# A hybrid diffusion layer on one core: transposes and half of the first projection chunk moved into the modulation, `w_out` loaded without waiting, the second half of the modulation spread out, the query projection led by token block 0, 36 expert rows ahead in place of 20

## The chip, the cores and the metric

The kernel runs on one core of one Trainium2 chip, in float32 throughout. The metric is the time of one execution on the device in microseconds (us), as the median of several runs. Addresses into this document: a name such as L720 is line 720 of the kernel before; the lines of the kernel after are named only where rows of its instruction order are shown.

## The reference, cut to what matters

One layer over 256 latent tokens (x) and 256 context tokens (ctx), width 2048. `silu` is applied to the two condition vectors, a product with `w_mod` (2048 x 12288) gives six modulation rows for each.

```python
mod = silu(c) @ w_mod + b_mod; mod_c = silu(c_ctx) @ w_mod + b_mod
sh1, sc1, ga1, sh2, sc2, ga2 = split(mod, 6)
pc = modulate(rmsnorm(ctx, g_norm_mix), csh1, csc1) @ w_in       # 2048 x 4128
p  = modulate(rmsnorm(x, g_norm_mix), sh1, sc1) @ w_in
four, qk, v, o, gates = split_proj(p, b_gate)
y_m, _ = mlstm_mix(silu(conv_latent(qk)), v, o, gates, g_mlstm, ctx_states)  # 8 heads
y = concatenate([fourier_mix(four, g_fourier), y_m]) @ w_out     # 2048 x 2048
x = x + ga1 * y
h2 = modulate(rmsnorm(x, g_norm_ffn), sh2, sc2)

def peer(xb):                                   # per block of 128 tokens
    q = (xb @ w_query).reshape(128, 8, 2, 128)  # 8 heads, 2048 x 2048
    s = einsum('thpd,hpnd->thpn', q, sub_keys)
    sv, si = top_k(s, 16)                       # then 16 x 16 candidates per head
    top_s, pos = top_k(cand, 16); idx = take_along_axis(cidx, pos)
    act = gelu(einsum('thkd,td->thk', expert_u[idx], xb))
    return einsum('thk,thkd->td', softmax(top_s) * act, expert_v[idx])
out = rmsnorm(x + ga2 * peer(h2), g_final)
```

The last part is the bulk of the traffic: each of 256 tokens picks 8 x 16 experts, and each pick is one row of 8 KB of `expert_u` and one of `expert_v`, 537 MB together.

## The kernel before, in words

Every engine has its own hand-written program (SyncE `sp`, GpSimd `pool`, ScalarE `act`, TensorE `pe`, VectorE `dve`), and semaphores tie them together: `wait_ge` blocks that engine's program in order, so what stands behind a wait waits too. Nothing reorders the work at run time.

1. **Modulation, first third.** `load_moda` (L263) brings the first 4096 columns of `w_mod` in 16 pieces of 2 MB into four buffers; a piece waits until the one four before it is used (`w_free`). `partial_mod` multiplies each piece on TensorE, with 32 output rows at a time in four column groups (L654); `columns_of_mod` (L662) turns the result into columns. ctx and x come between the pieces, ScalarE sums their squares, VectorE scales them (`norm_tokens`).
2. **Transposes and H.** After the last piece, 16 transposes of 512 tokens (L682) go through PSUM; ScalarE (L451) and VectorE (L982) modulate them into `H`, which holds all tokens with the channels on partitions.
3. **Projection.** `w_in` is used in 8 chunks of 512 columns, each as two halves of the contraction (`kh`), 2 MB each, on two buffers `W[0]`, `W[1]`. Ahead of it stand the gates, 16 matmuls of 104 rows (L690). Chunks 3, 2, 4, 5 (L714, L716, L720) run straight through; the other four are cut in halves and laid between the heads of the mLSTM. Meanwhile VectorE computes the other 16 chunks of the modulation for x alone: `modb(m)` is 16 multiply-adds over a 4 MB chunk of `w_mod` (L929), which GpSimd loads into `W[2]`, `W[3]`; TensorE sums its 128 rows (L699, `reduce_modb`), and `modb_out` adds the bias. 12 of the 16 are done before the scans (`MODB_LATE`), with the convolutions between them, 4 beside `w_out`.
4. **mLSTM.** For each head TensorE does half a chunk of projection, `values(h-1)` (L773), `scores(h)` (L755); VectorE `diagonals`, `weigh`, `divide` (L1122), ScalarE the exponentials. Then `positions` (L795) and `channels` (L807) do the Fourier group.
5. **w_out.** SyncE waits for `y_ready` (L284) before it loads the first piece of `w_out`. TensorE transposes y (L831), then four chunks of 64 matmuls for both token blocks (L846); VectorE adds to x. Then the keys are transposed (L860), `h2` of both blocks is normed (L1206, L1209) and transposed (L868).
6. **Query.** Four chunks n of `w_query`, 64 matmuls each for both blocks together (L883), then the scores of two heads (L893). `pick(g, n)` on VectorE finds the 16 experts of a head of a token block (g is 0 to 15; 0 to 7 are block 0). The `w_query` pieces are loaded by SyncE (L253), each into the half buffer that was just used.
7. **Experts.** One rank r (0 to 255) is 16 ranks per pick. `gather_u(r)` (L374, an indirect DMA from GpSimd, 1 MB) brings 128 rows of `expert_u`, `dot(r)` on VectorE (L1273) multiplies them with h2, `weight_of(r)` on ScalarE makes a diagonal of the weights, and TensorE adds 128 rows of `expert_v` under it (L905, 4 matmuls of 512 columns, 8 instructions). `LEAD` ranks of U are gathered, on `EARLY` = 5 buffers, before the first V; the first V waits for `w_free` 48 and `score_psum` 8, that is for the whole query stage, because V's buffers are those of `w_query` and its sums lie in the same PSUM banks. From there two V go with one U until U is `LAG` = 4 ahead, then one with one, on 6 U and 7 V buffers.

In TensorE's rows a float32 matmul stands as two instructions (16 matmuls are x32).

## Time and profile before

| | |
|---|---|
| median of 3 runs | 2081.48 us (2077.37 to 2081.89) |
| the profiled execution: its own time, its span | 2078.71 us, 2076.7 us |
| TensorE busy | 1669.7 us (80%) |
| VectorE busy | 1111.1 us (54%) |
| ScalarE, GpSimd busy | 389.0 us, 669.2 us |
| moved by DMA | 723.54 MB, mean 348 GB/s |
| TensorE clock, mean granted | 0.969 |

The span is what the trace covers, from the first to the last instruction; times in the trace are counted from its start. Busy shares are means over stages with different limits, so the stages have to be read one by one. A granted clock of 1.00 is 2.4 GHz. The rows that matter stand in a section of their own below.

### The profile page before, as it was taken

To read this page: it belongs to the slowest core of one execution; us is meant where nothing else is said; L and a number is where in the kernel's file an instruction comes from. 1 tells how busy PE (TensorE), PEld (TensorE's weight loads), DVE (VectorE), ACT (ScalarE), POOL (GpSimd) and SP (SyncE) were. 2 spreads that over 40 slices of the span, in tenths; PEclk is the share of its full clock that TensorE was granted. 3 is DMA by queue.
4 is the path that set the end of the run, shared out by engine and by line. 5 is a ranking of instruction groups with operands and counts; after the bars stand their busy time and mean duration, and the time that the engine had idled before them with its cause. 6 is when DMAs were issued, how large, how long until landed. Compare 5 with 4: busy or idle time off the path is not lost.

```text
span 2076.7 us, 13923 instructions
## 1 busy us (share of the span) xinstructions
PE 1669.7 (80%) x4609; PEld 782.8 (38%) x4609; DVE 1111.1 (54%) x1856; ACT 389.0 (19%) x1126; POOL 669.2 (32%) x577
## 2 busy tenths in 40 slices
PE   4599999999699978998777777777777777777776
PEld 1155544556444767333222223222232232222222
DVE  0177996234454284164646646646647556556443
ACT  1110002113200102122212122122123122122111
POOL 1011100000000052554445345355354464454430
PEclk8799999999899999999999999999999999999999
DMA  9978887231766395999999999999999999999996
GB/s 379 408 286 314 309 301 270 96 107 62 262 245 222 122 360 235 420 402 423 423 422 424 423 424 423 423 423 424 423 423 421 424 423 423 423 423 423 423 423 252
DMA packets 136759, 723.54 MB, mean 348 GB/s; under 512 B 10202, under 2 KB 10538, under 8 KB 69619
## 3 DMA queue, kind: packets, MB, share of 16 engines
q0 software_dynamic: 92784, 614.83, 72.0%
q1 hardware_dynamic: 43744, 107.78, 14.1%
q8 instruction: 36, 0.59, 0.1%
q14 instruction: 33, 0.26, 0.0%
q10 hardware_dynamic: 162, 0.08, 0.0%
HBM read 720.52 MB, written 2.13 MB: 348 GB/s over the span
## 4 chain that ended last, share of the span: by engine, by line
DMA 42%; PE 33%; DVE 12%; POOL 8%; issue 3%; ACT 1%; DVEq 0%; SPq 0%; POOLq 0%; ACTq 0%
DMA ring<-in_expert_u,acc 24%; PE ps L720 11%; DMA qh<-in_expert_u,acc 8%; PE ps L846 5%; POOL ring L374 5%; PE ps L883 5%; DMA ring<-in_w_mod 4%; DVE ring L1273 3%; PE ps L714 3%; PE ps L905 3%; DMA ring<-in_expert_v,acc 2%; DMA ring<-in_w_query 2%; DMA modrow<-in_expert_v,acc 1%; PE ps L716 1%; POOL VX L374 1%
## 5 line engine op out<-in xcount | busy, mean ns | idle before, releaser
L905 PE MATMUL ps<-ring,wg 128*128 128x512 f32 x1184 | 545.1, 605 | 178.1 <-DMA ring<-in_expert_v,acc 177.7
L1273 DVE SCALAR_TENSOR_TENSOR ring<-ring,A 128x2048 f32<-128x2048 f32 x174 | 397.0, 2292 | 334.3 <-DMA ring<-in_expert_u,acc 334.0
L905 PEld LDWEIGHTS ps<-ring,wg 128*128 128x128 f32 x1184 | 216.0, 191 | 506.0 <-issue 270.2
L374 POOL DMA_INDIRECT ring<-in_expert_u,acc x174 | 216.8, 1246 | 446.5 <-DVE ring L1273 337.3
L905 PE MATMUL ps<-H,wg 128*128 128x512 f32 x576 | 266.7, 607 | 81.7 <-DMA H<-in_expert_v,acc 81.7
L604 ACT ACTIVATE wg<-K,VX 128x128 f32<-128x128 f32 x256 | 102.8, 402 | 711.8 <-PE ps L905 707.4
L720 PE MATMUL ps<-ring,H 128*128 128x512 f32 x512 | 223.4, 595 | 1.2 <-ACT VX L473 1.2
L374 POOL DMA_INDIRECT ring<-in_expert_v,acc x148 | 177.1, 1196 | 69.2 <-issue 43.6
L905 PEld LDWEIGHTS ps<-H,wg 128*128 128x128 f32 x576 | 105.2, 191 | 242.5 <-issue 134.4
L929 DVE SCALAR_TENSOR_TENSOR acc<-ring,vec,acc 128x512 f32<-128x512 f32 x240 | 180.5, 752 | 21.6 <-DMA ring<-in_w_mod 13.3
L905 PE MATMUL ps<-modrow,wg 128*128 128x512 f32 x288 | 133.6, 607 | 39.4 <-DMA modrow<-in_expert_v,acc 39.4
L324 POOL DMA_DIRECT2D ring<-in_w_mod x32 | 28.8, 899 | 365.9 <-DVE acc L929 265.7
L720 PEld LDWEIGHTS ps<-ring,H 128*128 128x128 f32 x512 | 96.1, 190 | 125.2 <-issue 123.1
L1273 DVE SCALAR_TENSOR_TENSOR VX<-VX,A 128x2048 f32<-128x2048 f32 x43 | 98.5, 2291 | 80.9 <-DMA VX<-in_expert_u,acc 80.8
L1273 DVE SCALAR_TENSOR_TENSOR qh<-qh,A 128x2048 f32<-128x2048 f32 x39 | 89.4, 2291 | 79.6 <-DMA qh<-in_expert_u,acc 79.6
L883 PE MATMUL ps<-H,ring 128*128 128x256 f32 x512 | 113.3, 383 | 13.9 <-DMA ring<-in_w_query 13.4
L846 PE MATMUL ps<-ring,H 128*128 128x512 f32 x256 | 112.4, 600 | 12.9 <-DMA ring<-in_w_out 12.9
L883 PEld LDWEIGHTS ps<-H,ring 128*128 128x128 f32 x512 | 98.0, 192 | 28.2 <-issue 12.3
L374 POOL DMA_INDIRECT VX<-in_expert_u,acc x43 | 64.6, 1503 | 121.3 <-DVE VX L1273 115.8
L905 PEld LDWEIGHTS ps<-modrow,wg 128*128 128x128 f32 x288 | 52.6, 192 | 119.8 <-ACT wg L604 60.9
L599 ACT ACTIVATE VX<-VX 128x1 f32<-128x1 f32 x256 | 51.4, 201 | 224.3 <-DVE ring L1273 147.6
L374 POOL DMA_INDIRECT H<-in_expert_v,acc x72 | 78.0, 1084 | 28.1 <-issue 21.0
(216 smaller groups left out, 1251.0 us busy)
## 6 DMA issues: line engine op xcount, KB each, us to landing
ring<-in_w_mod POOLq DMA_DIRECT2D x32, 2048.0 KB, 8.7
ring<-in_w_mod SPq DMA_DIRECT2D x16, 2048.0 KB, 21.3
ring<-in_w_in SPq DMA_DIRECT2D x16, 2048.0 KB, 11.7
ring<-in_w_out SPq DMA_DIRECT2D x8, 2048.0 KB, 11.0
ring<-in_w_query SPq DMA_DIRECT2D x8, 2048.0 KB, 11.5
ring<-in_expert_u,acc POOLq DMA_INDIRECT x174, 26.2
ring<-in_expert_v,acc POOLq DMA_INDIRECT x148
B<-in_ctx SPq DMA_DIRECT2D x2, 1024.0 KB, 25.5
```

Of the source, the lines that this page charges most:

```text
L324: pool.dma_start(W[2 + kh], wm[kh * KH * P:(kh + 1) * KH * P, bass.ds(m * CH + 2 * D, CH)].rearrange("(k p) n -> p k n", p=P)).then_inc(m_ ...
L374: nc.gpsimd.indirect_dma_start(rows_, None, table, bass.IndirectOffsetOnAxis(ap=eidx[:, rank:rank + 1], axis=0)).then_inc(loaded, 16)
L599: link(nc_a.activation(act_t[:, r:r + 1], dots[:, r:r + 1], ACT.Gelu_apprx_tanh))
L604: nc_a.activation(diag[:, r % 4, :], ident, ACT.Copy, scale=wgt[:, r:r + 1]).then_inc(S["diag_ready"], 1)
L714: ins = mm(bank, W[kh][:, k, j * P:(j + 1) * P], H[:, kk, :], **flags)
L716: ins = mm(bank[:, 0:T], W[kh][:, k, j * P:(j + 1) * P], H[:, kk, T:2 * T], **flags)
L720: ins = mm(bank, H[:, kk, b * P:(b + 1) * P], W[kh][:, k, :], **flags)
L846: ins = mm(ps[:, 2 * par + b, :], yT[:, kk, b * P:(b + 1) * P], W[kh][:, k, :], start=kk == 0, stop=kk == KB - 1)
L883: ins = mm(ps[:, 2 * (n % 2) + j // 2, (j % 2) * T:(j % 2 + 1) * T], W[kh][:, k, j * P:(j + 1) * P], h2T[:, kk, :], start=kk == 0 and j % ...
L905: ins = mm(ps[:, 4 * b + n, :], diag[:, r % 4, :], v_rows[r % V_SLOTS][:, n * CH:(n + 1) * CH], start=k == 0, stop=k == BLOCK_RANKS - 1, s ...
L929: ins = v.scalar_tensor_tensor(out=a, in0=W[2 + kh][:, k, :], scalar=s, in1=a, op0=ALU.mult, op1=ALU.add)
L1273: v.scalar_tensor_tensor(out=rows_u, in0=rows_u, scalar=1.0, in1=A[:, r // BLOCK_RANKS, :], op0=ALU.mult, op1=ALU.mult, accum_out=dots[:, ...
```

## The change

All of it is in the order of work; what is computed is the same.

- **Front.** The first third of the modulation is computed in another column order (shift and scale of the first 1024 channels first), so that `H` of the first eight channel blocks can be made while the second half still loads. TensorE then has transposes and `project_early` between the pieces: the first half (`kh` 0) of chunk 3 of `w_in`, whose 2 MB are loaded into `KT` and `qh` between `w_mod` pieces 7 and 8. The gates are computed in four column groups of 32 rows and summed by one more matmul.
- **Modulation, rest.** 8 chunks of `modb` ahead of the scans in place of 12; 3.5 chunks go as halves between `weigh(h)` and `divide(h)` of heads 0 to 6, a half behind them, 4 beside `w_out` as before.
- **w_out.** Its first two pieces are loaded as soon as the projection is done (`w_free` 32). TensorE begins with the half of the contraction that the mLSTM fills, ahead of the wait for `y_ready`. The last chunk is done for token block 0 first, then the keys are transposed, then block 1.
- **Query.** Block 0 is normed and modulated by itself, its two first heads are projected one by one with the tokens on the output rows (then transposed), and scored and picked before block 1 is there. Chunks 1 to 3 are as before, with `kh` 1 first.
- **Experts.** `LEAD` is 36 in place of 20; near the end `lag_behind` lets V come from 4 to 1 behind U.

```diff
-REDUCE_BEHIND = [1, 4, 6, 10, 15, 19, 22, 24, 26, 28, 31]
...
+REDUCE_BEHIND = [7, 9, 13, 17, 20, 23, 26, 29]
...
-LEAD = 20
+LEAD = 36
...
+CLOSING = 24
...
-MODB_EARLY, MODB_LATE = 1, 12
+MODB_SCAN, MODB_LATE = 8, 12
...
+def lag_behind(u):
+    return LAG if u < RANKS - CLOSING else LAG - (u - (RANKS - CLOSING)) // (CLOSING // LAG)
...
+        WE = [KT[:], qh[:].rearrange("p a b t -> p (a b t)").rearrange("p (k n) -> p k n", k=4)]
...
+            c0 = W_IN_CHUNKS[0] * CH
+            for i in range(2):
+                sp.dma_start(WE[i], wi[4 * i * P:4 * (i + 1) * P, c0:c0 + CH].rearrange(
+                    "(k p) n -> p k n", p=P)).then_inc(S["ld_we"], 16)
+            for piece in range(8, 4 * MODA_N):
+                load_moda(piece)
+            sp.wait_ge(S["w_free"], 14)
+            load(1, wi, 1, bass.ds(W_IN_CHUNKS[0] * CH, CH))
...
-            sp.wait_ge(S["y_ready"], 1)
-            for base, src in ((32, w_out[0]), (40, w_query[0])):
-                with sp.Fori(0, 4) as n:
-                    for kh in range(2):
-                        sp.wait_ge(S["w_free"], n * 2 + (base + kh - 1))
-                        load(kh, src, kh, bass.ds(n * CH, CH))
+            sp.wait_ge(S["w_free"], 32)
+            for kh in HALVES:
+                load(kh, w_out[0], kh, slice(0, CH))
+            for n in range(1, 4):
+                for i, kh in enumerate(HALVES):
+                    sp.wait_ge(S["w_free"], 32 + 2 * n + i - 1)
+                    load(kh, w_out[0], kh, slice(n * CH, (n + 1) * CH))
...
-            load_from(1, MODB_LATE + 1)
+            load_from(1, MODB_SCAN + 1)
             pool.dma_start(gy[:, 0:FW], g_fourier.to_broadcast([P, FW])).then_inc(S["ld_gy"], 16)
             pool.dma_start(gy[:, FW:D], g_mlstm.to_broadcast([P, FW])).then_inc(S["ld_gy"], 16)
+            load_from(MODB_SCAN + 1, MODB_LATE)
...
+            pool.wait_ge(S["score_psum"], 10)
             for i in range(LEAD - LAG):
                 gather_u(LEAD + i)
                 gather_v(2 * i)
                 gather_v(2 * i + 1)
-            for r in range(2 * (LEAD - LAG), RANKS - LAG):
-                gather_u(r + LAG)
-                gather_v(r)
-            for r in range(RANKS - LAG, RANKS):
-                gather_v(r)
+            r = 2 * (LEAD - LAG)
+            for u in range(r + LAG, RANKS):
+                gather_u(u)
+                while r + lag_behind(u) <= u:
+                    gather_v(r)
+                    r += 1
+            gather_v(RANKS - 1)
...
+            def project_early(first, last):
+                for step in range(first, last):
+                    j, k = step // KH, step % KH
+                    if j == 0:
+                        wait_ht(k)
+                    if step == 0:
+                        pe.wait_ge(S["ld_we"], 32)
+                    ins = mm(ps[:, 1 + j, :], WE[k // 4][:, k % 4, j * P:(j + 1) * P], H[:, k, :],
+                             start=k == 0, stop=False)
+                    if step == 4 * KH - 1:
+                        ins.then_inc(S["w_free"], 1)
...
+            transpose_x(0)
+            transpose_x(1)
+            columns_of_mod(1).then_inc(S["modcol_psum"], 1)
+            transpose_x(2)
+            partial_mod(2, 0)
+            for k in range(3, 6):
+                transpose_x(k)
+            partial_mod(2, 1)
+            for k in range(6, 8):
+                transpose_x(k)
+            project_early(0, 4)
+            partial_mod(2, 2)
+            project_early(4, 8)
+            partial_mod(2, 3)
+            project_early(8, 12)
+            pe.wait_ge(S["mod_ready"], 1)
...
+            project_early(15, 18)
+            partial_mod(3, 2)
+            project_early(18, 21)
+            partial_mod(3, 3)
+            transpose_x(8)
+            project_early(21, 24)
+            columns_of_mod(3).then_inc(S["modcol_psum"], 1)
+            transpose_x(9)
+            transpose_x(10)
+            project_early(24, 26)
...
+                pe.wait_ge(S["ld_wg"], 16)
+                for k in range(KB):
+                    g = 32 * (k % 4)
+                    ins = mm(ps[g:g + 32, 0, :], wg[:, k, :], H[:, k, :], start=k < 4,
+                             stop=k >= KB - 4)
...
+                mm(ps[0:NG, 0, :], gate_sel, gate_parts, start=True, stop=True
...
+                    if (i, kh, j) == (0, 1, 0):
+                        gate_parts_of_projection()
+                    if (i, kh, j) == (0, 1, 1):
+                        sum_gates()
...
+                if h >= 2 and h % 2 == 0:
+                    reduce_modb(MODB_SCAN + h // 2 - 1)
...
+            for i in range(KB // 2):
+                transpose_y(i)
+            pe.wait_ge(S["yT_ready"], KB // 2)
+            project_out(0, 0)
+            reduce_modb(MODB_LATE - 1)
+            pe.wait_ge(S["y_ready"], 1)
+            for i in range(KB // 2, KB):
+                transpose_y(i)
             pe.wait_ge(S["yT_ready"], KB)
...
+            for n in range(3):
+                if n >= 1:
+                    project_out(n, 0)
+                project_out(n, 1)
+                reduce_modb(MODB_LATE + n)
+            project_out(3, 0, (0,))
+            project_out(3, 1, (0,)).then_inc(S["out_tb0"], 1)
+            reduce_modb(MODB_LATE + 3)
...
+            project_out(3, 0, (1,))
+            project_out(3, 1, (1,))
...
+            def query_head(b, h, first, last):
+                for step in range(first, last):
...
+                    ins = mm(ps[:, h, 0:T], h2T[:, kk, b * P:(b + 1) * P],
+                             W[kh][:, k, h * T:(h + 1) * T], start=step == 0, stop=step == KB - 1)
...
+            pe.wait_ge(S["out_free"], 6)
+            query_head(0, 0, 0, KB)
+            pe.wait_ge(S["out_free"], 8)
+            transpose_h2(1, 0)
+            transpose_h2(1, 1)
+            query_columns(0, 0)
+            query_head(0, 1, 0, 4)
+            head_scores(0, 0)
+            query_head(0, 1, 4, KB)
...
+            query_head(1, 0, 0, 4)
+            head_scores(0, 1)
+            query_head(1, 0, 4, KH)
+            query_head(1, 1, 0, KH).then_inc(S["w_free"], 1)
+            query_head(1, 0, KH, KB)
+            query_head(1, 1, KH, KB)
+            query_columns(1, 0).then_inc(S["w_free"], 1)
+            head_scores(1, 0)
+            query_columns(1, 1)
+            head_scores(1, 1)
...
+                if h >= 2 and h % 2 == 0:
+                    modb_out(MODB_SCAN + h // 2 - 1)
+                if h < MH - 1:
+                    modb_half(MODB_SCAN + h // 2, h % 2)
                 divide(h)
...
+            modb_half(MODB_LATE - 1, 1)
...
+            dve.wait_ge(S["out_tb0"], 1)
+            add_mixed(3, 0)
+            modb_out(MODB - 1)
+            dve.wait_ge(S["g2_ready"], 1)
+            dve.wait_ge(S["ld_sh2"], 16)
+            modulate(0)
+            dve.wait_ge(S["w_free"], 40)
+            add_mixed(3, 1)
+            modulate(1)
...
+                if g == 0:
+                    dve.wait_ge(S["score_ready"], 5)
+                if g == SOFT_FIRST - 2:
+                    dve.wait_ge(S["score_ready"], 10)
+                if g + 2 < TB * PH:
                     pick(g + 2, g + 2)
```

How TensorE's order changes at the front. Before, behind the last `w_mod` piece (L654, ring) the columns (L662), then the 16 transposes (L682, B is ctx, A is x), the gates (L690), the sum of a `modb` (L699), then chunk 3 (L714):

```order
L654 MATMUL ps<-ring,acc 32x512 x32
L662 MATMUL ps<-K,VX 128x2 x16
L682 MATMUL ps<-K,B 128x128 x2
L682 MATMUL ps<-K,A 128x128 x2
...
L690 MATMUL ps<-H,wg 104x512 x16
L699 MATMUL ps<-acc,K 32x512
L714 MATMUL ps<-H,ring 128x512 x16
```

After, from the first early projection on (L774, weights in KT and qh), with the `w_mod` pieces (L742) and a set of columns (L751) between; the lower rows are the end of the early work, the first piece of chunk 3's second half (L861) and the gates (L828):

```order
L774 MATMUL ps<-H,KT 128x512 x4
L742 MATMUL ps<-ring,acc 32x512 x8
L774 MATMUL ps<-H,qh 128x512 x4
L742 MATMUL ps<-ring,acc 32x512 x8
L774 MATMUL ps<-H,KT 128x512 x4
L751 MATMUL ps<-K,VX 128x2 x8
L742 MATMUL ps<-ring,acc 32x512 x8
L774 MATMUL ps<-H,qh 128x512 x3
...
L774 MATMUL ps<-H,qh 128x512
L861 MATMUL ps<-H,ring 128x512 x8
L828 MATMUL ps<-H,wg 32x512 x16
```

The 32 matmuls of the first half have moved from behind the transposes to between the pieces of `w_mod` 10 to 15, and 16 matmuls of 104 rows have become 16 of 32 rows.

From the transposes of y to the first query chunk, TensorE before: L831 transposes y, L846 is `w_out`, L852 sums a `modb`, L860 transposes the keys, L868 h2, L883 is the query projection, L893 scores:

```order
L831 MATMUL ps<-K,A 128x128 x32
...
L846 MATMUL ps<-ring,H 128x512 x32
...
L852 MATMUL ps<-acc,K 32x512
...
L860 MATMUL ps<-K,gy 128x128 x16
L868 MATMUL ps<-K,A 128x128 x32
L883 MATMUL ps<-H,ring 128x256 x64
L893 MATMUL ps<-modrow,qh 128x128 x8
```

After: L980 transposes y, L992 is `w_out`, L844 sums a `modb`, L1020 transposes the keys, L1031 h2, L1053 projects one head of one block:

```order
L980 MATMUL ps<-K,A 128x128 x16
L992 MATMUL ps<-ring,H 128x512 x16
L844 MATMUL ps<-acc,K 32x512
L980 MATMUL ps<-K,A 128x128 x16
L992 MATMUL ps<-ring,H 128x512 x16
...
L992 MATMUL ps<-ring,H 128x512 x16
L844 MATMUL ps<-acc,K 32x512
L1020 MATMUL ps<-K,gy 128x128 x16
L992 MATMUL ps<-ring,H 128x512 x16
L1031 MATMUL ps<-K,A 128x128 x16
L1053 MATMUL ps<-ring,H 128x256 x16
```

What follows on TensorE, block 1's h2 (L1031) and block 0's second head, with the query of head 0 turned (L1061) and scored (L1071):

```order
L1031 MATMUL ps<-K,A 128x128 x8
L1061 MATMUL ps<-K,qtok 128x128 x2
L1053 MATMUL ps<-ring,H 128x256 x4
L1071 MATMUL ps<-modrow,qh 128x128 x2
L1053 MATMUL ps<-ring,H 128x256 x12
L1031 MATMUL ps<-K,A 128x128 x8
```

Half a chunk of `w_out` now stands between the two halves of y's transposes, the keys' transposes and one block's h2 stand around the last half chunk, and the first scores come behind 20 query matmuls in place of 64.

## Rows read from the trace of the kernel before

**Rows 1.** The page, part 2: the span in 40 slices of 51.9 us.
```profile
GB/s 379 408 286 314 309 301 270 96 107 62 262 245 222 122 360 235 420 402 423 423 422 424 423 424 423 423 423 424 423 423 421 424 423 423 423 423 423 423 423 252
```

**Rows 2.** Windows: length, busy by engine (PE, PEld, DVE, ACT, POOL), clock, DMA share, GB/s.
```profile
90.00:104.00 14.00, 9.21 (x48) 1.81 (x48) 0.00 (x0) 0.00 (x0) 0.00 (x0) 0.64 1.03 401
...
1000.00:2000.00 1000.00, 741.74 (x1600) 290.85 (x1600) 585.51 (x919) 220.37 (x663) 480.53 (x400) 0.99 1.01 423
```

**Rows 3.** Timeline of TensorE at the front: start, busy us, operation [idle before].
```profile
54.79 1.95 PE L654 MATMUL ps<-ring,acc 128*32 128x512 f32 x16 [1.83 <-DMA ring<-in_w_mod]
...
100.88 3.27 PE L654 MATMUL ps<-ring,acc 128*32 128x512 f32 x16 [2.41 <-DMA ring<-in_w_mod]
...
119.42 13.95 PE L690 MATMUL ps<-H,wg 128*104 128x512 f32 x32 [1.26 <-ACT H L451]
...
134.28 14.00 PE L714 MATMUL ps<-H,ring 128*128 128x512 f32 x32
...
192.84 7.50 PE L716 MATMUL ps<-H,ring 128*128 128x256 f32 x34
```

**Rows 4.** Timeline of TensorE, the half chunk ahead of the heads.
```profile
340.90 13.97 PE L720 MATMUL ps<-ring,H 128*128 128x512 f32 x32 [1.21 <-ACT VX L473]
354.80 0.44 PE L738 MATMUL ps<-K,gsb 40*128 40x40 f32 x4
```

**Rows 5.** Timeline of VectorE in a head, after the heads, beside w_out.
```profile
393.40 0.16 DVE L1122 COPY small<-ps 128x2 f32<-128x2 f32 x1 [10.14 <-PE ps L773]
...
527.30 0.25 DVE L1156 RECIPROCAL st<-st 128x16 f32<-128x16 f32 x1 [15.13 <-ACT st L541]
...
640.85 11.78 DVE L929 SCALAR_TENSOR_TENSOR acc<-ring,vec,acc 128x512 f32<-128x512 f32 x15
```

**Rows 6.** Timeline of TensorE from the Fourier stage to the last scores.
```profile
494.58 3.70 PE L795 MATMUL ps<-K,A 128*128 128x512 f32 x8
...
531.93 6.24 PE L831 MATMUL ps<-K,A 128*128 128x128 f32 x32 [4.32 <-DVE A L1160]
...
551.12 29.23 PE L846 MATMUL ps<-ring,H 128*128 128x512 f32 x64 [12.94 <-DMA ring<-in_w_out]
...
684.84 27.89 PE L883 MATMUL ps<-H,ring 128*128 128x256 f32 x128 [0.52 <-ACT H L573]
...
758.92 15.76 PE L883 MATMUL ps<-H,ring 128*128 128x256 f32 x64 [12.13 <-DMA ring<-in_w_query]
...
822.00 2.05 PE L893 MATMUL ps<-modrow,qh 128*128 128x128 f32 x16 [1.16 <-ACT qh L583]
```

**Rows 7.** Timeline of VectorE and GpSimd in the query stage.
```profile
715.71 0.29 DVE L1234 COPY QT<-H 128x256 f32<-128x256 f32 x1 [34.82 <-ACT H L589]
...
727.07 0.29 DVE L1234 COPY QT<-H 128x256 f32<-128x256 f32 x1
...
751.54 2.29 DVE L1273 SCALAR_TENSOR_TENSOR ring<-ring,A 128x2048 f32<-128x2048 f32 x1 [0.96 <-DMA ring<-in_expert_u,acc]
...
754.78 2.29 DVE L1273 SCALAR_TENSOR_TENSOR ring<-ring,A 128x2048 f32<-128x2048 f32 x1 [0.94 <-DMA ring<-in_expert_u,acc]
...
803.34 2.29 DVE L1273 SCALAR_TENSOR_TENSOR VX<-VX,A 128x2048 f32<-128x2048 f32 x1 [1.04 <-DMA VX<-in_expert_u,acc]
...
727.90 1.02 POOL L374 DMA_INDIRECT ring<-in_expert_u,acc  x1 [51.65 <-DVE acc L1257]
...
824.82 0.94 POOL L374 DMA_INDIRECT ring<-in_expert_u,acc  x1 [32.53 <-PE ps L893]
```

**Rows 8.** Windows of the query stage and the end, columns as in group 2.
```profile
738.00:748.00 10.00, 7.63 (x42) 6.42 (x40) 9.30 (x11) 2.24 (x4) 6.38 (x3) 1.00 1.02 416
...
808.00:818.00 10.00, 10.00 (x48) 8.81 (x47) 0.00 (x0) 0.00 (x0) 0.00 (x0) 1.00 0.00 0
...
2049.00:2067.00 18.00, 17.41 (x40) 7.52 (x40) 2.81 (x7) 3.11 (x7) 0.00 (x0) 1.00 0.23 96
```

**Rows 9.** Timeline of TensorE, its last work on V rows.
```profile
2052.92 13.90 PE L905 MATMUL ps<-ring,wg 128*128 128x512 f32 x32
```

574 lines of the change are left out of this document (341 added, 233 removed).

## Prediction

> **What bounds the kernel now.** I read the page's slices first [rows 1], then windows, then each engine's timeline where slices sit below the plateau. The plateau is 423 GB/s, from slice 17 to the end: the experts' rows. There TensorE is busy 742 of 1000 us and VectorE 586 [rows 2], so transfers alone set the pace: a row of 1.0486 MB each 1.0486 / 0.423 = 2.48 us. Everything ahead is a chain with other limits. The first 104 us move `w_mod` at 401 GB/s, TensorE working 9.2 of 14 us at clock 0.64 [rows 2] and waiting for each piece (1.83, 2.41 us) [rows 3]. From 119 to 349 TensorE projects almost without a pause [rows 3, 4]; the heads run to 494.6; then come Fourier, `w_out`, query [rows 6]. DMA is far below its rate there, so shorter TensorE work shortens the chain. Two holes stand in the query stage: the first gather starts at 727.90, when the first pick ends, and after the 20th dot (803.34) DMA stands at 0 GB/s until the last scores release V at 824.82 [rows 7, 8].
>
> **Front.** Two MB more on the full queue are 2.1 / 0.401 = 5 us: last piece at 106 by DMA. But TensorE now has more than it waits for. From 62, when the first half is known, to the last piece stand: eight products of pieces (8 x 1.95 = 16), 21 early matmuls (0.87 each from 14.00 for 16, [rows 3]: 18), eight transposes (16 of them and the columns fill 104.15 to 119.42, [rows 3]: about 0.9 each, 7), two sets of columns (estimate: 2 each as a piece, 4), turns (6, estimate): 51, so it is through at 113, not 104. Behind them the last columns, eight transposes and 11 matmuls (19) give 132. Chunk 3's second half is 32 x 0.87 = 27.8; the gates, 16 matmuls of 32 rows in four column groups, cost what two pieces of the modulation do (2 x 1.95 = 3.9, [rows 3]) in place of 13.95; their sum 0.9; a reduce 1.0. Chunk 3 ends at 166 against 192.84 [rows 3]: **-27**. Bounds: -33 if TensorE catches each piece; -7 if the low clock holds: at the 3.27 / 1.95 of row 100.88 the 51 and 19 become 86 and 32, less what waits filled. The reduces change places: one fewer ahead of the heads, three more in them (1.04 each): +2. VectorE has 8 chunks of `modb` before the scans, four fewer (12.6 each, 16/15 of 11.78, [rows 5]), so it follows a TensorE that is 27 early. The heads hide the halves: VectorE idles 10.14 before `divide` [rows 5], a half costs 6.3 and every second time about 0.7 for `modb_out`, at most 7.0; the last half fits the 15.13 idle [rows 5]: cost 0. Were that cover gone, it would be 7 x 6.3 + 3 x 0.7 = 46. So `positions` starts at 494.58 - 25 = 469.6; call it t0.
>
> **w_out.** Before, y's transposes start at t0 + 37.4 and the load's landing stalls TensorE 12.94 [rows 6]. With pieces loaded early and half a chunk ahead of the second transposes, the 12.94 and the 4.32 ahead of the transposes go. A chunk is 27.8 + 1.04: starting at t0 + 41, chunks end at +73.5, +102.3, +131.2; block 0 of the last at +145.1; the reduce behind it waits for VectorE until about +147.6, as its last `modb` is behind the adds (11.78 each, [rows 5]); keys to +152, block 1's half to +166, block 0's transposes to +169.3. The query starts at **t0 + 170.5** where it was 684.84, t0 + 190.3 [rows 6]: -20. Norming block 0 needs 2.4 us of VectorE behind +147.6 and lies under the 14 us of block 1. Sixteen matmuls of 256 columns (27.89 / 64 each, 7), copies, turns and scores (5.5, estimate: a chunk now has 3.2 of them, 2.05 for scores, and transposes more) and a pick of 11.36 (715.71 to 727.07, [rows 7]) put the first gather at t0 + 194.4 = 664 against 727.9: **-64**.
>
> **Query against 36 U rows.** What those 64 us buy hangs on this stage. Six later pieces of `w_query` (12.6 MB) now compete with 36 rows of U (37.7 MB). While both queues are full DMA moves 416 GB/s [rows 8], and a row of U lands every 3.24 us (751.54 to 754.78, both waiting for DMA [rows 7]): U has 1.0486 / 3.24 = 0.324, `w_query` the other 0.09, about a fifth. In that regime TensorE waited 12.13 for a half chunk [rows 6]. Half a chunk of work takes 13.95, a piece at 0.09 MB/us needs 23, so now TensorE waits at nearly every piece. The sum of bytes is the better bound: 50.3 / 0.41 = 123 us from t0 + 194; the same sum on before gives (21.0 + 8.4) / 0.41 = 72 from 728, so 800 against a last dot at 803.34. To this come 10 us in which U stands still: VectorE waits inside its program for the fifth scores, and with it the dots that free U's buffers; and 17 for the half chunk and scores behind the last piece (13.9 + 2.05 + turns). V starts at t0 + 345 = 815 against 824.82: **-10**. Bounds: if `w_query` gets half the bytes, it is VectorE's 36 dots (2.29) and picks that end last, t0 + 333 (803); if it is starved below the fifth, all pieces land after the U rows, t0 + 374 (844).
>
> In the Trainium skill, "DMA: Bandwidth & Descriptors", section "Queues, rings and completion order", each DMA engine takes turns between the queues it has work for, a packet at a time. By an equal turn of equal packets `w_query` would keep half the bytes and V would start at 803; the trace has it at a fifth and stands against an equal share in bytes, though turns of packets of unequal size (pieces of 2 KB runs, rows of 8 KB) would fit it.
>
> **Experts.** Sixteen rows fewer stand behind the first V: 16 x 2.48 = **-39.7**. They cost no more than 2.48 there, since TensorE's 3.5 per V row stays under the pair's 4.95. At the end the last bytes land about 2053 (96 GB/s x 18 us = 1.73 MB in the last window, 4 us, [rows 8]) while TensorE still has four rows (2052.92, 13.90, [rows 9]). With `lag_behind` the last V rows come interleaved with the last U, not four in a row at 2.48 against TensorE's 3.5, so one or two remain: 13.7 becomes 5 to 6, **-8** (bounds -5, -9).
>
> **Sum.** -10 - 39.7 - 8 = -57.7. The profiled execution has a span of 2076.7 and its own time 2078.71, 2.8 under the median. 2076.7 becomes 2019, own time 2021; on the median 2081.48 - 57.7 = **2024**. The likeliest case's own range: bounds of the front (+8, -4), of the share (-8, +8) and of the end (+3, -1), not all at once: 2012 to 2037.
>
> **Rivals.**
> A. `w_query` is not starved: pieces issued while dots hold U back slip through, as U has only five buffers. V at 803, 12 earlier: 2012. For it: some stretches of VectorE are picks without dots. Against: row spacing 3.24 in the trace [rows 7]. By the turns told of in the Trainium skill, "DMA: Bandwidth & Descriptors", section "Queues, rings and completion order", this is the case that would come.
> B. The front gives little. Interleaved products, transposes and 512-column matmuls are dense but switch forms, and TensorE may stay at the 0.64 of 90 to 104 [rows 2]; pieces then free late and `w_mod` arrives late. Gain 7 in place of 25: 18 to 20 less: 2043. For it: the clock there. Against: it rose to full by 119.42 (13.95 for 16 matmuls, [rows 3]) once work was dense. Switching by itself is spoken against by the Trainium skill, "TensorEngine Tiling (Array Packing)", section "Key Properties": a change of tiling mode drains TensorE. No row here prices a drain apart; the price of B is the clock's alone.
> C. `w_query` starved behind the U queue. LEAD at 36 then costs all it saves: V at 844, 19 after the 824.82: +19 - 39.7 - 8 = -28: 2053. For it: the 12.13 stall with only 20 rows [rows 6]. Against: U can't queue more than five rows.
> D. Slower. The halves between `weigh` and `divide` wait for their piece of `w_mod`, loaded by GpSimd into two buffers that free one half at a time. `divide(h)` then comes late, head by head, and `values` and `scores` behind it. Room is left for 10.14 - 7.0 = 3.1 per head [rows 5]; a piece later than this by x costs 7x, and over 57.7 / 7 = 8.2 per head, 11.3 late in all, the change is lost: 12 gives 7 x (12 - 3.1) = 62, 2086, and with 14 it is 2100. Against: a 2 MB piece needs 5 us of a DMA that is mostly idle there (62 to 262 GB/s, [rows 1]), and a head lasts (494.58 - 354.80) / 8 = 17.5 [rows 4, 6].
> E. No change: pieces in the heads come 11.3 late, D's point, and take back what the rest gives: within 4 of 2081.
>
> **Chances.** Forecast 0.57, A 0.12, B 0.18, C 0.08, D 0.03, E 0.02. What a measurement can tell is 0.2%, 4 us. Faster by more than that: 0.95, same 0.02, slower 0.03. The range leaves out D, E, C and the far edges: 2003 (A's 2012 less the bounds of front and end) to 2048 (B's 2043 and 5 of its bounds).
>
> **What would show it.** Right: chunk 3's second half ends near 166, half chunk ahead of the heads near 327, no head longer than now; `positions` at 470; no wait for `w_out`; query from 640; first gather near 664; TensorE waiting 8 to 25 us for several `w_query` pieces, with U rows 3.24 apart; first V near 815 with some idle DMA ahead; 423 GB/s from there; TensorE under two rows behind at the end. Wrong: a clock under 0.8 from 60 to 130 (B), the first V before 806 or after 835 (A, C), VectorE waiting for DMA inside the heads (D). The weakest term is the V start, since it rests on a share seen in one row spacing and one stall.

## The result and the profile after

The changed kernel takes 2022.32 us (median of 4 runs, 2021.78 to 2025.9) against 2079.43: a ratio of 0.9729, interval 0.971 to 0.9747, 57 us less, where 57.7 less was forecast. The profiled execution has 2022.52 us, its span 2020.7, which is 56.0 less than before.

First TensorE's timeline after (start, busy us, operation, idle before and who ended it), which answers to [rows 3], [rows 4] and [rows 6]. L742 are the `w_mod` pieces, L774 the early projection, L763 the transposes, L861 and L863 chunks 3 and 2, L828 the gates, L945 `positions`, L992 `w_out`, L1053 and L1108 the query, L1120 its scores:

```profile
79.25 3.60 PE L774 MATMUL ps<-H,KT 128*128 128x512 f32 x8
...
111.28 0.44 PE L763 MATMUL ps<-K,B 128*128 128x128 f32 x2
...
126.03 7.03 PE L861 MATMUL ps<-H,ring 128*128 128x512 f32 x16
132.99 3.64 PE L828 MATMUL ps<-H,wg 128*32 128x512 f32 x32
...
159.19 7.17 PE L863 MATMUL ps<-H,ring 128*128 128x256 f32 x32
...
322.95 0.43 PE L886 MATMUL ps<-K,gsb 40*128 40x40 f32 x4
...
465.66 3.70 PE L945 MATMUL ps<-K,A 128*128 128x512 f32 x8
...
506.85 14.00 PE L992 MATMUL ps<-ring,H 128*128 128x512 f32 x32 [0.52 <-ACT H L595]
...
632.40 3.72 PE L1053 MATMUL ps<-ring,H 128*128 128x256 f32 x16 [0.83 <-ACT H L613]
...
690.38 15.63 PE L1108 MATMUL ps<-H,ring 128*128 128x256 f32 x64 [18.98 <-DMA ring<-in_w_query]
713.85 15.84 PE L1108 MATMUL ps<-H,ring 128*128 128x256 f32 x64 [7.84 <-DMA ring<-in_w_query]
...
789.67 15.48 PE L1108 MATMUL ps<-H,ring 128*128 128x256 f32 x64 [12.01 <-DMA ring<-in_w_query]
806.32 2.05 PE L1120 MATMUL ps<-modrow,qh 128*128 128x128 f32 x16 [1.16 <-ACT qh L672]
```

The reader is to see three things. Chunk 3 ends at 159.19 and the heads begin at 322.95, with no idle time between the pieces from 79 on. Ahead of `w_out` the wait for its load is gone. And TensorE's idle time named `in_w_query` has grown to 38.8 us in three waits, where the kernel before had 13.4 in two (12.13 and 1.23).

VectorE and GpSimd in the query stage, answering to [rows 7]. L1528 is the dot, L1489 begins a pick, L413 is a gather:

```profile
699.01 2.29 DVE L1528 SCALAR_TENSOR_TENSOR ring<-ring,A 128x2048 f32<-128x2048 f32 x1 [0.95 <-DMA ring<-in_expert_u,acc]
...
702.26 2.29 DVE L1528 SCALAR_TENSOR_TENSOR ring<-ring,A 128x2048 f32<-128x2048 f32 x1 [0.94 <-DMA ring<-in_expert_u,acc]
...
732.67 0.29 DVE L1489 COPY QT<-H 128x256 f32<-128x256 f32 x1 [15.34 <-ACT H L678]
...
659.41 1.01 POOL L413 DMA_INDIRECT ring<-in_expert_u,acc  x1 [40.48 <-DVE acc L1512]
...
746.60 2.74 POOL L413 DMA_INDIRECT ring<-in_expert_u,acc  x1 [28.06 <-DVE ring L1528]
...
811.78 0.94 POOL L413 DMA_INDIRECT ring<-in_expert_u,acc  x1 [22.78 <-DVE ring L1528]
```

Windows after, columns as in [rows 2]: one in the front, one full stretch of the query stage, two stretches in which DMA has a hole, and the experts:

```profile
90.00:104.00 14.00, 14.00 (x71) 6.45 (x68) 1.29 (x2) 0.00 (x0) 0.00 (x0) 1.00 1.03 408
693.00:713.00 20.00, 13.02 (x59) 11.01 (x58) 14.47 (x13) 0.00 (x0) 5.61 (x6) 0.93 1.02 414
727.00:747.00 20.00, 18.84 (x95) 16.48 (x94) 12.71 (x43) 2.25 (x4) 0.40 (x1) 1.00 0.49 178
791.00:811.00 20.00, 16.20 (x78) 13.80 (x77) 18.42 (x48) 4.23 (x12) 0.00 (x0) 0.96 0.29 120
1000.00:2000.00 1000.00, 754.34 (x1643) 297.56 (x1644) 561.71 (x865) 218.47 (x667) 482.81 (x395) 1.00 1.01 422
```

U rows are 3.25 us apart beside `w_query`, as before. The first gather is at 659.41 in place of 727.90, yet the first gather behind the stage is at 811.78 in place of 824.82: 68.5 us earlier at the start, 13.0 at the end. DMA has two holes in the stage. The first comes where VectorE waits for the fifth scores (15.34) and then makes a pick: GpSimd asks for no U row for 28.06 us. The second stands ahead of the experts. What ends it is another wait than before: the row at 811.78 is U row 36, and it waits for a dot (DVE L1528), while the last scores were ready at 806.32 + 2.05 = 808.37. In the kernel before, the row at 824.82 waited for the scores.

The end, TensorE's last row after, answering to [rows 9]:

```profile
2003.65 7.10 PE L1132 MATMUL ps<-ring,wg 128*128 128x512 f32 x16 [1.26 <-DMA ring<-in_expert_v,acc]
```

Two rows are left where four were.

### The profile page after: what moved, and what is told of

It is laid out like the page before. It is cut to its first block, busy times and chain, and to the rows that moved or that the text cites. A ratio compares the mean times of both kernels' runs of the same rounds, so it can differ in the third digit from the quotient of the medians.

```text
span 2020.7 us, 13865 instructions
## 1 busy us (share of the span) xinstructions
PE 1647.9 (82%) x4619; PEld 774.8 (38%) x4619; DVE 1112.4 (55%) x1862; ACT 381.8 (19%) x1124; POOL 695.9 (34%) x572
## 3 DMA queue, kind: packets, MB, share of 16 engines
q1 hardware_dynamic: 43760, 107.82, 14.2%
## 4 chain that ended last, share of the span: by engine, by line
DMA 43%; PE 31%; DVE 12%; POOL 9%; issue 3%; SPq 1%; ACT 1%; DVEq 0%; POOLq 0%
DMA ring<-in_expert_u,acc 17%; PE ps L867 11%; DMA ring<-in_expert_v,acc 10%; DMA qh<-in_expert_u,acc 7%; POOL ring L413 6%; PE ps L992 4%; PE ps L1132 3%; DVE ring L1528 3%; DMA ring<-in_w_query 3%; DMA ring<-in_w_mod 2%; DMA H<-in_expert_v,acc 2%; PE ps L774 1%; PE ps L863 1%; PE ps L861 1%; POOL VX L413 1%
## 5 line engine op out<-in xcount | busy, mean ns | idle before, releaser
L1528 DVE SCALAR_TENSOR_TENSOR ring<-ring,A 128x2048 f32<-128x2048 f32 x177 | 404.1, 2293 | 381.7 <-DMA ring<-in_expert_u,acc 381.4
L413 POOL DMA_INDIRECT ring<-in_expert_u,acc x177 | 243.7, 1377 | 393.2 <-DVE ring L1528 323.4
L1132 PE MATMUL ps<-H,wg 128*128 128x512 f32 x576 | 262.5, 600 | 67.0 <-DMA H<-in_expert_v,acc 67.0
L413 POOL DMA_INDIRECT ring<-in_expert_v,acc x148 | 175.4, 1185 | 106.1 <-PE ps L1132 62.2
L1528 DVE SCALAR_TENSOR_TENSOR VX<-VX,A 128x2048 f32<-128x2048 f32 x43 | 98.5, 2292 | 86.6 <-DMA VX<-in_expert_u,acc 86.5
L1528 DVE SCALAR_TENSOR_TENSOR qh<-qh,A 128x2048 f32<-128x2048 f32 x36 | 82.5, 2292 | 92.7 <-DMA qh<-in_expert_u,acc 92.7
L1108 PE MATMUL ps<-H,ring 128*128 128x256 f32 x384 | 88.8, 395 | 38.8 <-DMA ring<-in_w_query 38.8
L992 PE MATMUL ps<-ring,H 128*128 128x512 f32 x256 | 111.6, 594 | 2.7 <-DMA ring<-in_w_out 1.4
L413 POOL DMA_INDIRECT H<-in_expert_v,acc x72 | 82.8, 1150 | 47.2 <-PE ps L1132 29.8
L413 POOL DMA_INDIRECT VX<-in_expert_u,acc x43 | 66.0, 1535 | 93.8 <-DVE VX L1528 87.1
L1108 PEld LDWEIGHTS ps<-H,ring 128*128 128x128 f32 x384 | 75.9, 199 | 50.9 <-DMA ring<-in_w_query 39.8
```

What stands on the lines that cost most here:

```text
L413: nc.gpsimd.indirect_dma_start(rows_, None, table, bass.IndirectOffsetOnAxis(ap=eidx[:, rank:rank + 1], axis=0)).then_inc(loaded, 16)
L992: ins = mm(ps[:, 2 * (n % 2) + b, :], yT[:, kk, b * P:(b + 1) * P], W[kh][:, k, :], start=part == 0 and k == 0, stop=part == 1 and k == KH ...
L1108: ins = mm(ps[:, 2 * (n % 2) + j // 2, (j % 2) * T:(j % 2 + 1) * T], W[kh][:, k, j * P:(j + 1) * P], h2T[:, kk, :], start=part == 0 and k ...
L1132: ins = mm(ps[:, 4 * b + n, :], diag[:, r % 4, :], v_rows[r % V_SLOTS][:, n * CH:(n + 1) * CH], start=k == 0, stop=k == BLOCK_RANKS - 1, s ...
L1528: v.scalar_tensor_tensor(out=rows_u, in0=rows_u, scalar=1.0, in1=A[:, r // BLOCK_RANKS, :], op0=ALU.mult, op1=ALU.mult, accum_out=dots[:, ...
```

## The experiments

Each has the changed kernel as its base (2022.32) and is quoted with its ratio to the kernel before, whose median in the three batches was 2078.61, 2078.35 and 2079.49; beside the base it was 2079.43, so a difference to the base has about 1 us of uncertainty from this alone. Each experiment has one trace.

**The number of U rows ahead.**

```diff
-LEAD = 36
+LEAD = 20
...
-SOFT_FIRST = 4
+SOFT_FIRST = 3
...
```

> The changed kernel with 20 rows of U ahead of the first V in place of 36 (the softmax work that hangs on the count moved with it), so this undoes the number alone. Theory (the rows are early traffic that costs w_query its share, and each later V row less costs 2.48 us): the first wait for w_query (19 us at 671 to 690) stays, the later ones (12.0 before the last half chunk) go, last scores near 794 instead of 808, then 16 rows more behind them, 16 x 2.48 = 40: about +25 us, 2047 us. Rival 1 (the start of V does not depend on the U rows at all): +40. Rival 2 (each early row pushes the start of V back by as much as it saves): 0.

Measured: 2046.7 us, ratio 0.9841 (0.9825 to 0.9858): 24 more than with 36. TensorE's timeline with 20 rows, the query chunks, then GpSimd's first gather behind the stage:

```profile
691.47 16.74 PE L1108 MATMUL ps<-H,ring 128*128 128x256 f32 x64 [19.05 <-DMA ring<-in_w_query]
714.96 16.94 PE L1108 MATMUL ps<-H,ring 128*128 128x256 f32 x64 [6.75 <-DMA ring<-in_w_query]
...
794.75 2.05 PE L1120 MATMUL ps<-modrow,qh 128*128 128x128 f32 x16 [1.16 <-ACT qh L672]
...
797.56 0.94 POOL L413 DMA_INDIRECT ring<-in_expert_u,acc  x1 [78.34 <-PE ps L1120]
```

The last scores come at 794.75 in place of 806.32, the first gather behind them at 797.56 in place of 811.78. So sixteen rows more cost the stage 14 us and save about 16 x 2.48 = 40 behind it; 14.2 + 24.4 is 38.6. Both rivals fall; the theory's number was 25.

The run shows one thing more. With the same 20 rows the stage lasts 797.56 - 660.41 = 137 us here and 824.82 - 727.90 = 97 in the kernel before. Of the 67.5 us by which the first gather is earlier, 27 are left at the stage's end. Block 0's first gather comes while six pieces of `w_query` are still to be loaded, where it was four, and TensorE waits 19.05 and 6.75 us for them. No run undoes the lead of block 0 by itself, so what it alone is worth stays open.

**The hole filled.** VectorE does 32 dots before it asks for the fifth scores, so the U rows do not stop there.

```diff
-                if g == 0:
+                if g == 1:
                     dve.wait_ge(S["score_ready"], 5)
+                    pick(2, 2)
...
-                if g + 2 < TB * PH:
+                if 1 <= g and g + 2 < TB * PH:
                     pick(g + 2, g + 2)
```

> The changed kernel, but VectorE does the dots of the second pick (rows 16 to 31) before it waits for the fifth scores and makes the third pick, so that the U rows do not stop at 717 to 746 us. Theory (what the hole loses in U rows it gives to w_query, and TensorE's chain ends last): the hole closes, but the wait ahead of the second chunk's second half comes back (some 8 us) and the last one shrinks; start of V 4 us earlier, bounds -10 to +6; about 2018 us. Rival (idle DMA is lost time wherever it stands): the 23 us of the hole come off, 2000 us.

Measured: 2021.33 us, ratio 0.9723 (0.9707 to 0.9739), not to be told from the base. Two of its windows, where the hole was and where it has one now, and TensorE's timeline:

```profile
717.00:746.00 29.00, 23.46 (x108) 20.04 (x107) 20.16 (x18) 2.25 (x4) 7.66 (x9) 0.94 1.02 414
766.00:780.00 14.00, 12.84 (x67) 11.20 (x67) 12.26 (x44) 2.25 (x4) 0.17 (x1) 1.00 0.39 126
```

```profile
735.33 15.77 PE L1108 MATMUL ps<-H,ring 128*128 128x256 f32 x64 [4.38 <-DMA ring<-in_w_query]
758.66 16.39 PE L1108 MATMUL ps<-H,ring 128*128 128x256 f32 x64 [7.56 <-DMA ring<-in_w_query]
...
807.05 2.05 PE L1120 MATMUL ps<-modrow,qh 128*128 128x128 f32 x16 [1.16 <-ACT qh L672]
```

DMA moves 414 GB/s through the old hole, and TensorE now waits 4.38 and 7.56 where it had waited for nothing; the 12.01 ahead of the last half chunk is gone. The last scores are at 807.05 against 806.32. In the hole `w_query` had come undisturbed; with the hole filled, its pieces come later.

The idle time of DMA did not go away, it moved: from 717 to 746 DMA moves 414 GB/s in place of 264, but from 766 to 780 it moves 126 where the changed kernel has 414, and from 659 to 812 the mean is 330 in both. So the rival falls, as U rows brought forward gained nothing. That idle DMA is worth nothing the run doesn't show.

**The share of `w_query`, by the size of its runs.**

```diff
-                    load(kh, w_query[0], kh, slice(n * CH, (n + 1) * CH))
+                    if n == 0:
+                        load(kh, w_query[0], kh, slice(n * CH, (n + 1) * CH))
+                    else:
+                        sp.dma_start(W[kh].rearrange("p k n -> p (k n)").rearrange(
+                            "p (k n) -> p k n", k=KH // 2),
+                            w_query[0][kh * FW:kh * FW + FW // 2, (n % 2) * FW:(n % 2 + 1) * FW]
+                            .rearrange("(k p) n -> p k n", p=P)).then_inc(w_ld[kh], 16)
```

> The changed kernel with the pieces of w_query for chunks 1 to 3 read as runs of 4 KB in place of 2 KB (1024 columns of half as many rows), same bytes to the same buffers; so TensorE gets other weights than the reference's in these chunks and the picks of twelve of the sixteen heads are others. Theory (the DMA engines take turns by transfers of one run, 2 KB of w_query against 8 KB of U, which is the fifth that the trace shows): with 4 KB the share becomes a third, U rows beside w_query are 3.8 us apart in place of 3.24, the first wait of TensorE shrinks from 19 to about 8 us and the start of V comes 8 to 15 earlier: 2010 us. Rival (the share goes by queue, whatever the size of the runs): spacing 3.24, 19 us, 2022.

Measured: 2010.94 us, ratio 0.9668 (0.9652 to 0.9684), 11 less than the base. The DMA view from 650 to 830, queues with their packets and bytes, first of the changed kernel, then with 4 KB runs:

```profile
q0 software_dynamic: 6090, 44.40, 60.3%
q1 hardware_dynamic: 6240, 12.58, 19.0%
```

```profile
q0 software_dynamic: 6714, 48.97, 66.8%
q1 hardware_dynamic: 3168, 12.58, 17.6%
```

And VectorE's, TensorE's and GpSimd's timeline with 4 KB runs:

```profile
687.14 2.29 DVE L1534 SCALAR_TENSOR_TENSOR ring<-ring,A 128x2048 f32<-128x2048 f32 x1 [1.62 <-DMA ring<-in_expert_u,acc]
...
691.08 2.29 DVE L1534 SCALAR_TENSOR_TENSOR ring<-ring,A 128x2048 f32<-128x2048 f32 x1 [1.63 <-DMA ring<-in_expert_u,acc]
...
682.76 30.14 PE L1114 MATMUL ps<-H,ring 128*128 128x256 f32 x128 [10.36 <-DMA ring<-in_w_query]
...
781.91 2.05 PE L1126 MATMUL ps<-modrow,qh 128*128 128x128 f32 x16 [1.16 <-ACT qh L678]
...
801.12 0.94 POOL L419 DMA_INDIRECT ring<-in_expert_u,acc  x1 [20.21 <-DVE ring L1534]
```

Half the packets carry the same 12.58 MB: 12.58 MB / 6240 is 2.0 KB a packet, 12.58 MB / 3168 is 4.0; U's queue has a mean of 7.3 KB, its rows being 8 KB. U rows move from 3.25 to 3.94 us apart, so U keeps 1.0486 / 3.94 = 0.266 of 0.417 MB/us and `w_query` 36%, where it had 22%. Turns of one packet each would give 4 / (4 + 8) = 33% and 2 / (2 + 8) = 20%, and so would turns of any equal number of packets. The first wait falls from 18.98 to 10.36. The rival, a share by queue alone, falls.

TensorE's last scores are 24 us earlier (781.91 in place of 806.32), but the whole kernel gains only 11, as the first gather behind the stage does (801.12 in place of 811.78). It waits for a dot of VectorE, long behind the scores.

**One queue for both.**

```diff
+QUERY_BEHIND = (4, 4, 12, 18, 21, 27)
...
-            for n in range(4):
+            for n in range(1):
...
+            query_piece = 2
             for r in range(LEAD):
                 gather_u(r)
+                for _ in range(QUERY_BEHIND.count(r)):
+                    n, i = query_piece // 2, query_piece % 2
+                    kh = HALVES[i]
+                    pool.wait_ge(S["w_free"], 40 + query_piece - 1)
+                    pool.dma_start(W[kh], w_query[0][kh * KH * P:(kh + 1) * KH * P,
+                                                     n * CH:(n + 1) * CH].rearrange(
+                        "(k p) n -> p k n", p=P)).then_inc(q_ld[kh], 16)
+                    query_piece += 1
...
```

> The changed kernel with the six pieces of w_query for chunks 1 to 3 issued by GpSimd between the gathers of U (behind U rows 4, 4, 12, 18, 21 and 27), in place of SyncE beside them. Theory (pieces lose against queued U rows because they take turns; in one queue each has the full rate in its place): the first piece lands near 678 in place of 690, the waits of 19, 8 and 12 shrink to under 10 together, the scores of the second chunk are there before VectorE asks for them, and the stage is bound by its bytes, 50.3 MB at 0.415 = 121 us from 659: start of V near 782 in place of 812, 1992 us (1988 to 2003). Rival (the waits are latency, or the work of TensorE ends last anyway): within 5 us of 2022.

Measured: 2014.75 us, ratio 0.9694 (0.9678 to 0.971): 8 less, not the 30 that was expected. TensorE's timeline, then GpSimd's:

```profile
681.28 29.81 PE L1119 MATMUL ps<-H,ring 128*128 128x256 f32 x128 [10.76 <-DMA ring<-in_w_query]
...
732.56 15.77 PE L1119 MATMUL ps<-H,ring 128*128 128x256 f32 x64 [4.45 <-DMA ring<-in_w_query]
...
770.18 15.77 PE L1119 MATMUL ps<-H,ring 128*128 128x256 f32 x64 [4.82 <-DMA ring<-in_w_query]
787.11 2.05 PE L1131 MATMUL ps<-modrow,qh 128*128 128x128 f32 x16 [1.16 <-ACT qh L683]
```

```profile
803.40 0.94 POOL L415 DMA_INDIRECT ring<-in_expert_u,acc  x1 [20.20 <-DVE ring L1539]
804.64 0.94 POOL L415 DMA_INDIRECT ring<-in_expert_v,acc  x1 [0.30 <-issue]
```

The waits of TensorE are 20.0 in place of 38.8 and the last scores stand at 787.11, 19 earlier. That part held. But GpSimd's program begins the experts with the gather of U row 36, which needs the buffer of row 35 and so waits for the dot of row 35; VectorE makes a pick between dots 31 and 32, and the wait lasts until 803.40. That is 8.4 us earlier than in the changed kernel, which is where the gain comes from. The bound had moved to a wait that the expectation had not looked at. The next two kernels test this reading.

**V rows first.**

```diff
+V_AHEAD = 6
...
+            for r in range(V_AHEAD):
+                gather_v(r)
+            r = V_AHEAD
             for i in range(LEAD - LAG):
                 gather_u(LEAD + i)
-                gather_v(2 * i)
-                gather_v(2 * i + 1)
-            r = 2 * (LEAD - LAG)
-            for u in range(r + LAG, RANKS):
+                while r < min(2 * (i + 1) + V_AHEAD, LEAD + i + 1 - LAG):
+                    gather_v(r)
+                    r += 1
+            for u in range(2 * LEAD - LAG, RANKS):
...
```

By itself on the changed kernel:

> The changed kernel, but when the query stage is over GpSimd issues six V rows first and only then the gather of U row 36, which waits for the dot of row 35; two V rows go with one U after that, as now. Theory (GpSimd's program stands in order, and in the changed kernel the first V rows stand behind a U gather that waits for VectorE from 808.4 to 811.8): DMA begins 3 us earlier, -3, 2019 us. Rival (the start is set by the scores alone): 0, and with the U rows later than V a loss of up to 5.

Measured: 2022.12 us, ratio 0.9724 (0.97 to 0.9747). The first V gather moved from 813.02 to 810.42, the last wait for a V row only from 2003.65 to 2003.26: too little to see, and the 3 us expected did not come. There the scores stood close ahead of the dot (808.37 against a gather at 811.78), so little was to be won. Where the rest of the 2.6 went is not settled.

Together with the one queue:

> The kernel with w_query issued by GpSimd between the U rows (2014.75) and in addition six V rows ahead of U row 36. Theory (there the scores were done at 789.2, but the first V stood behind a gather that waited until 803.4 for the dot of row 35, as VectorE made a pick first): DMA resumes near 790, 13 earlier, of which the U rows that VectorE still owes cost some: -10, 2005 us (2000 to 2009). Rival (VectorE's dots set the end of the stage and V rows fetched earlier only wait in their buffers): 2012 to 2015.

Measured: 2003.47 us, ratio 0.9628 (0.9604 to 0.9651), 11 less than the one queue alone. GpSimd's timeline:

```profile
791.43 0.94 POOL L416 DMA_INDIRECT ring<-in_expert_v,acc  x1 [6.71 <-PE ps L1135]
...
804.38 0.94 POOL L416 DMA_INDIRECT ring<-in_expert_u,acc  x1 [1.68 <-DVE ring L1543]
```

V is asked for at 791.43, on the scores, while U row 36 still waits until 804.38. The first V gather of the one queue alone was at 804.64, 13.2 later. So the reading holds: the order of GpSimd's program had cost 11 us there. This is the fastest of all kernels run, 19 us under the changed one. V rows first together with 4 KB runs was not run.

**The early load of `w_out`.**

```diff
-            sp.wait_ge(S["w_free"], 32)
+            sp.wait_ge(S["y_ready"], 1)
             for kh in HALVES:
                 load(kh, w_out[0], kh, slice(0, CH))
```

> The changed kernel, but the first pieces of w_out are again loaded only when y_ready has come; undoes the early load alone. Theory (the load lies on the chain as it did before, 12.94 us): y_ready comes near 506.5, so TensorE, which begins w_out at 506.85, waits until the first piece has landed, 10 to 15 us, and everything behind it is that much later: +13, 2035 us. Rival (the order of the halves has made the load's time free anyway, or a later query stage gives it back): under 4.

Measured: 2048.85 us, ratio 0.9855 (0.9838 to 0.9871): 26.5 more, twice the expected. TensorE's timeline, then the DMA issues from 500 to 535 with KB and median us to landing:

```profile
529.41 16.18 PE L992 MATMUL ps<-ring,H 128*128 128x512 f32 x32 [22.54 <-DMA ring<-in_w_out]
```

```profile
ring<-in_w_mod POOLq DMA_DIRECT2D x2, 2048.0 KB, 14.2
ring<-in_w_out SPq DMA_DIRECT2D x2, 2048.0 KB, 31.1
B<-in_x POOLq DMA_DIRECT2D x1, 2048.0 KB, 20.0
...
gy<-in_sub_keys POOLq DMA_DIRECT2D x1, 1024.0 KB, 23.2
```

The piece shares the engines with x and the keys, as in the kernel before, and now also with two `w_mod` pieces asked for 5 us ahead and with the rows of a norm. From 507 to 530 all of it moves at 397 GB/s. From the piece's issue to the first matmul on it were 551.12 - 535.63 = 15.5 us before and are 529.41 - 506.76 = 22.7 here. So 7.2 of the 9.6 us by which the wait is longer are a slower load; the rest is that TensorE has less to do in the meantime (half of y's transposes). That the other transfers make the load slow is a reading of the rates, and no run takes them away.

**The early projection.** In short, the seven calls that stand between the pieces become one behind them:

```diff
-            project_early(0, 4)
             partial_mod(2, 2)
-            project_early(4, 8)
...
             partial_mod(3, 3)
+            project_early(0, 21)
```

> The changed kernel with the 21 early projection matmuls that stand between the last six pieces of w_mod moved behind the last piece; transposes, packed gates and column order stay. Theory (they fill time in which TensorE waits for w_mod, 21 x 0.87 = 18, and give back at most 2 to 3 since the pieces are then used a little earlier): +16, 2038 us, and the granted clock from 76 to 104 us is 0.6 to 0.8 in place of 1.00. Rival (the front is bound by the 40 MB of w_mod and VectorE behind it takes back what TensorE gains): under 5.

Measured: 2041.68 us, ratio 0.9818 (0.9801 to 0.9834), 19 more. TensorE's timeline and a window:

```profile
142.49 7.03 PE L856 MATMUL ps<-H,ring 128*128 128x512 f32 x16
```

```profile
90.00:104.00 14.00, 9.12 (x64) 3.68 (x64) 0.65 (x2) 0.00 (x0) 0.00 (x0) 0.88 1.03 409
```

The second half of chunk 3 begins at 142.49 in place of 126.03: 16.5. For the clock the expectation said 0.6 to 0.8 from 76 to 104; that stretch has 0.88, too.

**The halves in the heads.**

```diff
-            def modb_half(m, kh):
+            def modb_half(m, kh, used=KH):
...
-                    modb_half(MODB_SCAN + h // 2, h % 2)
+                    modb_half(MODB_SCAN + h // 2, h % 2, 1)
```

> The changed kernel with each half of a modulation chunk in the heads 0 to 6 cut from 8 multiply-adds to the first one (the loads stay), so that ga2 and sh2 are in part other numbers than the reference's; the same for the halves outside the heads, all of which are shortened only if they lie in the heads. It prices the cover of the halves: theory (they lie in idle time before the divide): within 3 of 2022. Rival (VectorE in the heads is on the path and the halves cost up to 5.5 each): 20 to 40 less.

Measured: 2023.45 us, ratio 0.9738 (0.9718 to 0.9757). The run computes `ga2` and `sh2` in part wrongly; only its time counts. From the heads' start (320.33) to `positions` (463.04) it is 142.71 us, in the changed kernel 465.66 - 322.95 = 142.71. The cover is complete.

**The lag at the end.**

```diff
-    return LAG if u < RANKS - CLOSING else LAG - (u - (RANKS - CLOSING)) // (CLOSING // LAG)
+    return LAG
...
-            gather_v(RANKS - 1)
+            for r in range(RANKS - LAG, RANKS):
+                gather_v(r)
```

> The changed kernel with V a constant 4 rows behind U to the end, the last four V rows in a row, as before. Theory (the end of TensorE is 13.7 behind the last byte in place of 7): +6, 2028 us (+4 to +8). Rival (the lag at the end costs nothing since the last U rows then come earlier): within 2.

Measured: 2026.03 us, ratio 0.9744 (0.9728 to 0.976), 3.7 more. Its last TensorE row:

```profile
2000.77 13.90 PE L1133 MATMUL ps<-ring,wg 128*128 128x512 f32 x32
```

It ends at 2014.67, the changed kernel at 2010.75, and both had their first V gather at 813.0. By the times alone the difference is not certain, since the intervals of the two ratios overlap; the traces show where it comes from, four rows at the end in place of two.

## Why the prediction was right, point by point

**Front (-27 by chunk 3's end, -25 by `positions`).** Measured 192.84 to 159.19, -33.7, and 494.58 to 465.66, -28.9: the far bound of the range for this term. The mechanism was right: `e2_early_behind` prices the filling at 16.5 of it on TensorE, the gates went from 13.95 to 3.64 and their sum of 1.02. The gates were not undone by a run of their own.

The mis-sized term is the 19 us behind the last piece, which took 14.75 (111.28 to 126.03). The prediction took 0.9 us for each transpose of 512 tokens from the stretch 104.15 to 119.42. But there the transposes followed each other 0.88 us apart only at first, and 0.43 apart at the end, two sets of columns (4.32) and a wait (1.26) stood in the same stretch, and the mean granted clock from 104 to 119 was 0.77. At 1.00 they follow each other 0.43 apart in the changed kernel, too.

TensorE was through with the pieces at 111.3, against 113 predicted. The low clock of rival B never came: 1.00 from 90 to 104, where it had been 0.64. What lifts it the runs do not separate: in that window TensorE was busy for 9.21 us before at 0.64 and for 9.12 in `e2_early_behind` at 0.88, so its busy time alone does not tell them apart.

Of the 33.7 us, 31.9 are left when the heads begin (354.80 to 322.95), as the half chunk ahead of them waits 2.19 us where it had waited 1.21, and takes 15.67 in place of 13.97. The heads took 142.7 against 139.8, which is the three sums moved there, as the prediction's sum had it (its sign "no head longer than now" had forgotten them).

**The halves in the heads (0).** Measured 0, by `e2_halves_free`. Rival D needed a late piece; none was.

**`w_out` (-20).** Measured t0 + 166.7 to the query, -23.5: TensorE waited for no piece of `w_out` but one, later, for 1.40 us. As to what the old wait would cost here, the prediction took the 12.94 of before; `e2_wout_wait` shows 22.5. The sum is not touched by it, but the early load was worth twice what was written.

**First gather (664).** Measured 659.4. The query began at 632.4 in place of 640.1, and from there to the first gather it took 27.0 us in place of 24, with a wait of 1.97 for `w_query` among them.

**The query stage (V starts at 815).** Measured 811.8, 152 us behind the first gather, predicted 151. The account holds: 3.25 us between U rows, waits of 18.98, 7.84 and 12.01. The two holes of DMA that the prediction put on top of the bytes, 10 and 17 us, are there: 20 us at 178 GB/s in place of 414 are 11.4 us of missing traffic, and 20 us at 120 are 14.2.

Some details were off. The waits came at three pieces of six, not at nearly every one: the other three were there in time, with U standing still from 717.61 to 746.60. Rival A had described this, though its gain did not come. U stood still longer, for 28.06 us of GpSimd and not 10, but `w_query` used a part of that. And TensorE did not end last: its scores were ready at 808.4, and the gather of U row 36 waited for a dot until 811.8. The prediction's 17 us behind the last piece were 18.7 (789.67 to 808.37), so the two ends lay 3 us apart. The prediction had VectorE's end only as a bound, at 803, and it was luck that this end cost no more here; in `e1_same_queue` and `e1_runs4k` it sets the time. `e1_fill` shows that the place of the first hole does not matter.

Rival A fell; `e1_runs4k` shows what decides it. What the prediction had taken from the trace as a fifth is the turn of as many packets on either side: 2 KB against 8. By the Trainium skill, "DMA: Bandwidth & Descriptors", section "Queues, rings and completion order", the turns go by packets. The runs agree in that the share follows the size of what the trace counts as a packet, which was one run here; how many of them one turn takes they do not show, since any equal number gives the same share.

**Experts (-39.7).** From the first gather of the stage to TensorE's last V row it is 1242.0 before and 1199.0 after, -43.0. The lag accounts for 3.9 (`e2_lag`), which leaves 39.1 for the 16 rows; `e1_lead20` gives 38.6.

**The end (-8).** Measured -3.9. This term was twice too large: the prediction let the last rows be there when DMA's bytes end. But the last wait for a V row ended at 2003.65, while DMA had moved nearly all of its bytes by 2000, as this window after shows:

```profile
2000.00:2010.00 10.00, 8.74 (x21) 3.72 (x20) 4.05 (x5) 2.66 (x6) 0.00 (x0) 1.00 0.07 29
```

29 GB/s for 10 us are 0.3 MB, some 0.7 us at the full rate. TensorE gets the row about 3 us behind nearly all of the bytes, and then does two, 7.10 us. Whether it waited for the row's last bytes is open, as some still trickle in: 131 GB/s from 2000 to 2001, 33 from 2003 to 2004.

So -13.0, -39.1 and -3.9 make -56.0, the difference of the spans, and the sum of -57.7 came out near it as errors of 3 to 4 us went both ways. That it came this near is luck; that it lay in the range is not.
